# Gate-up weights of a mixture-of-experts kernel in blocks of 4 MB with runs of 32 KB per partition

## The chip, the cores and the metric

One core of a Trainium2 chip runs the whole program. The metric is the time of one execution on the device, in microseconds (us). "Before" and "after" are the kernel without and with the change.

## The reference, cut to what matters

One transformer layer on 256 tokens of 1024 features, all in float32. A token mixer (convolution branch, attention branch, gates, a merge) comes first; it ends in `x`. Then a mixture of experts reads the normalised `x`:

```python
logits = h @ w_router + b_router            # 32 experts
top_logits, top_idx = lax.top_k(logits, 4)  # 4 of them per token
gu = xb @ w_gate_up[e] + b_gate_up[e]       # (tokens, 1024) @ (1024, 2048)
glu = minimum(gu[:, ::2], 7); lin = clip(gu[:, 1::2], -7, 7)
act = glu * sigmoid(1.702 * glu) * (lin + 1)
y = act @ w_down[e] + b_down[e]             # (tokens, 1024) @ (1024, 1024)
```

The results are weighted, summed over a token's four experts, added to `x` and normalised. Every expert is worked on, so 8 MB of gate-up weights and 4 MB of down weights are read for each of the 32.

## The kernel before

**Stages.** Until about 290 us the mixer runs: TensorE multiplies weight chunks that SP streams through staging buffers. Then the experts follow one after the other, in pairs (`pair(m, last)`, L994, with `p` 0 and 1; expert number `i = 2m + p`). A program would add more rounds over the experts if one had over 64 tokens; register `final` (L536, L992) holds the last pair's number, 15 here.

**One expert on TensorE.** Gate-up (L999 to L1017) walks the 1024 features in eight steps `k` of 128. Two steps share one slot of 2 MB, so four slots j = 0 to 3 hold an expert's gate-up weights; after each slot the counter `up_used` goes up by one. Then come, for every second expert, the sum of two experts' rows into the output (`scatter`, L982), the gathering of the next expert's tokens (L955), its bias (L933), transposes of the activations (L1039) and of the gathered rows (`turn_gathered`, L963), and the product with the down weights (L1045 to L1055) from slots 4 and 5, with `down_used` counted. Which feature stands in which partition and step is the order of `PAIRS` (L66): the transposes L862, L967 and L694 read every second column, and `load_slot` (L432) gives partition p two neighbouring rows of the weights, a run of 16 KB.

**Slots.** There are ten slots of 128 partitions by 16 KB (L219): four for the gate-up weights of even experts, four for those of odd ones (`slot`, L372), two for down weights. They lie over buffers of the mixer, so the first loads wait until these are no longer needed (`EARLY`, L119, and L520 to L534). TensorE waits for a slot by its own semaphore (`wait_slot`, L376). ScalarE and VectorE work beside it (sigmoid L1250, clamps L1682 and L1684).

**The order of SP's queue.** SP issues every weight load and waits before each for the slot to be free. All transfers go through the one queue in the order of issue. `first_of_second(i)` (L547) issues the four gate-up loads of expert i + 2, each once expert i has used that slot; `rest_of_next(i)` (L538) issues the two down loads of expert i + 1, once expert i has used the down slots. For experts 0 to 16 the gate-up loads are issued first (L555 to L561), from 17 on the down loads (L562 to L569):

```python
first_of_second(2 * CATCH_UP, 0)      # CATCH_UP = 8
rest_of_next(2 * CATCH_UP, 0)
rest_of_next(2 * CATCH_UP + 1, 1)
first_of_second(2 * CATCH_UP + 1, 1)
```

**Other lines that the text speaks of.** ScalarE's queue loads the gate-up biases (L1205, four transfers, each 32 rows of 2 KB into 32 partitions) and the down biases (L1208, 32 rows of 4 KB into partitions 0 to 31). VectorE computes `final` in L1633 to L1639 and signals `routed`. Early in the program, VectorE computes the scalar `lam` in L1300 to L1303.

## Time and profile before

| | |
|---|---|
| median of three runs | 1215.8 us (1212.63 to 1217.0) |
| the profiled execution, its own time | 1212.78 us |
| its span in the profile | 1211.0 us |
| mean granted TensorE clock | 0.995 of full |

The page of the profile describes the one profiled execution, engine by engine, and the views behind it answer for a stretch, a line or an engine. In the stretches view each line is one stretch: its length, then busy us and number of instructions of TensorE's matmuls (PE), its weight loads (PEld), VectorE (DVE), ScalarE (ACT) and GpSimd (POOL), then the granted clock, the busy share of the 16 DMA engines (packets that lie across the ends of a stretch can lift it over 1), and GB/s. The span is 1.8 us shorter than that execution's time.

### The profile page before, as it was taken

What the parts mean: (1) busy time and instruction counts of PE and PEld (TensorE: products, weight loads), DVE (VectorE), ACT (ScalarE), POOL (GpSimd) and SP (SyncE); (2) the same over time, 40 slices, a digit from 0 to 9 for tenths busy, and PEclk for the clock granted to TensorE, in tenths of its full rate; (3) what the DMA queues carried; (4) which work ended last, traced back from release to release, by engine and by line L of the source; (5) the groups of instructions that cost most, each with busy time, mean ns of one, the idle gap of its engine ahead of it and who ended that gap; (6) DMA issues with size and microseconds to landing.
All of it is one profiled execution on the core that took longest, in us unless ns stands there. A gap on an engine that the chain in (4) does not pass through costs nothing.

```text
span 1211.0 us, 15215 instructions
## 1 busy us (share of the span) xinstructions
PE 1148.4 (95%) x6027; PEld 534.1 (44%) x6027; DVE 409.5 (34%) x795; ACT 208.7 (17%) x333; POOL 19.7 (2%) x40
## 2 busy tenths in 40 slices
PE   5999999999999999999999998989999999999997
PEld 4787899985333333333333332323333333333332
DVE  4447746663232222222222222222232222222222
ACT  4346543341011010101010101010110101010001
POOL 1000010000000000000000000000000000000000
PEclk9999999999999999999999999999999999999999
DMA  9997565798999999999999999999999999999994
GB/s 338 395 386 280 182 230 167 255 398 369 397 428 430 427 430 426 431 426 429 428 429 428 429 428 429 427 382 421 426 432 425 431 426 431 426 430 427 430 426 206
DMA packets 59394, 470.55 MB, mean 389 GB/s; under 512 B 5871, under 2 KB 11196, under 8 KB 32742
## 3 DMA queue, kind: packets, MB, share of 16 engines
q1 hardware_dynamic: 56644, 467.99, 93.5%
q10 hardware_dynamic: 2722, 2.16, 0.6%
q8 instruction: 20, 0.33, 0.1%
q14 instruction: 8, 0.07, 0.0%
HBM read 469.08 MB, written 1.06 MB: 388 GB/s over the span
## 4 chain that ended last, share of the span: by engine, by line
PE 65%; DMA 29%; DVE 2%; ACT 1%; SPq 1%; issue 1%; DVEq 0%; POOLq 0%; POOL 0%; ACTq 0%
PE ps L1014 19%; DMA expert<-in_w_down 16%; PE ps L783 15%; PE ps L1052 15%; DMA expert<-in_w_gate_up 12%; PE ps L988 4%; PE ps L959 2%; PE ps L727 1%; PE ps L658 1%; PE ps L940 1%; PE ps L1039 1%; ACT r_work L1254 1%; SPq L440 1%; DVE r_v L1691 1%; DMA ada_first<-in_w_ada 1%
## 5 line engine op out<-in xcount | busy, mean ns | idle before, releaser
L1014 PE MATMUL ps<-expert,r_work 128*64 128x512 f32 x2048 | 451.7, 594 | 12.3 <-DMA expert<-in_w_gate_up 11.3
L1014 PEld LDWEIGHTS ps<-expert,r_work 128*64 128x64 f32 x2048 | 146.5, 137 | 300.1 <-issue 280.1
L1052 PE MATMUL ps<-expert,r_work 128*64 128x512 f32 x1024 | 233.4, 606 | 24.1 <-DMA expert<-in_w_down 15.9
L1682 DVE TENSOR_SCALAR r_v<-ps 128x512 f32<-128x512 f32 x32 | 22.1, 692 | 371.3 <-PE ps L1014 371.3
L1052 PEld LDWEIGHTS ps<-expert,r_work 128*64 128x64 f32 x1024 | 72.8, 139 | 162.7 <-issue 136.9
L1250 ACT ACTIVATE r_v<-r_v 128x512 f32<-128x512 f32 x32 | 20.2, 630 | 713.8 <-DVE r_v L1682 713.8
L1702 DVE TENSOR_TENSOR r_work<-ps,r_gb 64x512 f32<-64x512 f32 x64 | 44.1, 689 | 169.5 <-PE ps L1052 169.0
L1364 DVE TENSOR_TENSOR w_lo<-stage,w_hi 128x2048 fp32r<-128x2048 f32 x36 | 82.2, 2289 | 55.9 <-ACT w_hi L1110 55.9
L783 PE MATMUL ps<-x_hi,w_hi 128*128 128x256 f32 x304 | 87.6, 288 | 0.0
L783 PE MATMUL ps<-x_lo,w_hi 128*128 128x256 f32 x304 | 86.0, 283 | 0.0
L783 PE MATMUL ps<-x_hi,w_lo 128*128 128x256 f32 x304 | 86.0, 283 | 0.0
L1110 ACT ACTIVATE w_hi<-stage 128x2048 fp32r<-128x2048 f32 x36 | 68.8, 1912 | 91.6 <-PE ps L783 68.9
L783 PEld LDWEIGHTS ps<-x_hi,w_hi 128*128 128x128 f32 x304 | 58.2, 191 | 11.6 <-issue 11.6
L959 PE MATMUL ps<-x_sb,r_work 128*64 128x512 f32 x256 | 61.2, 599 | 0.0
L988 PE MATMUL ps<-r_work 128*128 128x512 f32 x128 | 59.2, 605 | 0.0
L1623 DVE TENSOR_TENSOR r_work<-ps,small 128x256 f32<-128x256 f32 x64 | 26.9, 421 | 93.0 <-PE ps L967 93.0
L783 PEld LDWEIGHTS ps<-x_lo,w_hi 128*128 128x128 f32 x304 | 58.3, 192 | 0.0
L783 PEld LDWEIGHTS ps<-x_hi,w_lo 128*128 128x128 f32 x304 | 58.2, 192 | 0.0
L988 PEld LDWEIGHTS ps<-r_work 128*128 128x128 f32 x128 | 23.0, 189 | 35.9 <-issue 35.9
L940 PE MATMUL ps<-r_cu,r_work 32*64 32x512 f32 x256 | 34.8, 613 | 0.0
L959 PEld LDWEIGHTS ps<-x_sb,r_work 128*64 128x64 f32 x256 | 16.9, 136 | 39.7 <-issue 39.0
L1691 DVE TENSOR_TENSOR r_v<-r_v 128x512 f32<-128x512 f32 x32 | 33.6, 1049 | 1.1
(219 smaller groups left out, 862.3 us busy)
## 6 DMA issues: line engine op xcount, KB each, us to landing
expert<-in_w_gate_up SPq DMA_DIRECT2D x128, 2048.0 KB, 26.9
expert<-in_w_down SPq DMA_DIRECT2D x64, 2048.0 KB, 20.4
stage<-in_w_in SPq DMA_DIRECT2D x24, 1024.0 KB, 5.6
stage<-in_w_ada SPq DMA_DIRECT2D x16, 1024.0 KB, 7.7
ada_first<-in_w_ada SPq DMA_DIRECT2D x16, 256.0 KB, 6.4
ada_first<-in_w_ada SPq DMA_DIRECT2D x8, 512.0 KB, 12.2
stage<-in_w_o_attn SPq DMA_DIRECT2D x4, 1024.0 KB, 7.7
stage<-in_w_merge SPq DMA_DIRECT2D x4, 1024.0 KB, 5.8
```

Source lines behind the costliest of these rows:

```text
L783: m = pe.matmul(out_ap, lhs, rhs, start=first, stop=last, skip_group_check=True)
L940: pe.matmul(ps[CAP * g:CAP * g + CAP, j, :], sel[rows_of], bgu[rows_of, :], start=True, stop=False)
L959: mm = pe.matmul(ps[CAP * half:CAP * half + CAP, 2, :], g_hot[:, t, :], x_sb[:, t, 512 * half:512 * half + 512], start=(t == 0), stop=(t = ...
L988: pe.matmul(ps[:, 4 + 2 * t + half, :], st[:, t * P:t * P + P], y2[:, 512 * half:512 * half + 512], start=False, stop=False, skip_group_ch ...
L1014: mm = pe.matmul(ps[CAP * g:CAP * g + CAP, j, :], xg[:, 2 * (k % 4) + k // 4, :], buf[:, col:col + 512], start=False, stop=(k == KD - 1))
L1052: mm = pe.matmul(ps[CAP * half:CAP * half + CAP, 3, :], aT[:, ch, CAP * g:CAP * g + CAP], expert[n][:, col:col + 512], start=(q == 0), sto ...
L1110: act.activation(w_hi[n % 2], src, ACT.Copy).then_inc(hi_ready, 1)
L1364: v.tensor_tensor(w_lo[n % 2], src, w_hi[n % 2], ALU.subtract).then_inc(lo_ready, 1)
L1623: own.done(v.tensor_tensor(dst[:, qs], src[:, qs], per_chunk(a2, qs), ALU.mult))
L1682: v.tensor_scalar(glu.rearrange("p (b n) -> p b n", b=2), gu[:, :, :, 0], LIMIT, None, ALU.min).then_inc(glu_ready, 1)
L1691: v.tensor_tensor(act_sb.rearrange("p (c n) -> p n c", c=4), lin.rearrange("p (n c) -> p n c", c=4), sig.rearrange("p (n c) -> p n c", c=4 ...
L1702: ins = v.tensor_tensor(y2[CAP * p:CAP * p + CAP, 512 * half:512 * half + 512], ps[rows_in, 3, :], g2b[rows_in, 512 * half:512 * half + 51 ...
```

## The change

Slots that lie side by side in memory are joined to five blocks of 32 KB per partition. The features are dealt by fours: partition p of a block holds four neighbouring rows, 32 KB in one run. `load_block` loads a block with two transfers of 2 MB, one to partitions 0 to 63, one to partitions 64 to 127; each counts up the semaphore of one of the two slots. TensorE waits for both before the first step of a block, except in the last pair of experts. Loads by single slots remain for the gate-up weights of experts 0 to 3, 18 to 21, 30 and 31; all others (22 experts, 44 blocks) come by blocks. The order of gate-up and down loads changes over experts 17 to 19, one slot per expert. The first ten loads keep their waits, but which of them stands behind which wait is new. `lam` is computed later in VectorE's program. SP reads a second register value, which VectorE prepares before `routed`.

```diff
-PAIRS = [slice(2 * P * (k // 2) + k % 2, 2 * P * (k // 2) + 2 * P, 2) for k in range(4)]
+FOURS = [slice(k, 4 * P, 4) for k in range(4)]
...
-EARLY = {11: 0, 28: 1, 33: 2}
+EARLY = {11: 2, 28: 0, 33: 1}
+REST = [6, 3, 4, 5, 7, 8, 9]
...
-        order = [o_xn, o_bias, o_bp, o_oh, o_q, o_gate + 8192, in_order[1], o_w[0], o_w[2], o_hh]
-        expert = [at(f"expert{n}", o, 2 * SLOT) for n, o in enumerate(order)]
+        order = [o_bias, o_bp, o_xn, o_q, o_gate + 8192, in_order[1], o_oh, o_w[0], o_w[2], o_hh]
+        blocks = [at(f"expert{n}", order[2 * n], 4 * SLOT) for n in range(len(order) // 2)]
+        expert = [blocks[n // 2][:, 2 * SLOT * (n % 2):2 * SLOT * (n % 2) + 2 * SLOT] for n in range(len(order))]
+        assert all(order[n + 1] == order[n] + 8 * SLOT for n in range(0, len(order), 2))
...
                 if j < UP_SLOTS:
-                    src = w_gate_up[0, e, 2 * P * j:2 * P * j + 2 * P, :].rearrange("(p k) n -> p (k n)", k=2)
+                    d = 4 * P * (j // 2)
+                    src = w_gate_up[0, e, d:d + 4 * P, :].rearrange("(p h k) n -> p h (k n)", h=2, k=2)[:, j % 2, :]
...
+            def load_block(b, e, parity):
+
+                d = 4 * P * b
+                src = w_gate_up[0, e, d:d + 4 * P, :].rearrange("(p k) n -> p (k n)", k=4)
+                for part in range(2):
+                    n, rows_of = slot(2 * b + part, parity), slice(64 * part, 64 * part + 64)
+                    sp.dma_start(blocks[slot(2 * b, parity) // 2][rows_of, :], src[rows_of]).then_inc(slot_landed[n], 16)
...
-            for j in range(len(EARLY), NSLOT + TWICE):
-                if j == 3:
+            for n in REST:
+                if n == 6:
                     wait_product(sp, WO1, 1)
-                elif j == 4:
+                elif n == 3:
                     sp.wait_ge(m_lo, 4)
-                elif j == 5:
+                elif n == 4:
                     sp.wait_ge(m_ready, 4)
                     sp.wait_ge(lo_ready, STAGE_LAST[0] + 1)
-                elif j == 6:
+                elif n == 5:
                     sp.wait_ge(lo_ready, STAGE_LAST[2] + 1)
-                elif j == 7:
+                elif n == 7:
                     sp.wait_ge(half_done, 2 * (len(CHUNKS) - 1))
                 else:
                     wait_product(sp, MG1, 1)
-                load_slot(j % NSLOT, j // NSLOT, j // NSLOT)
+                load_slot(n % NSLOT, n // NSLOT, n // NSLOT)
             sp.wait_ge(routed, 1)
             final = sp.value_load(last_pair[0:1, 0:1], min_val=E // 2 - 1, max_val=ROUNDS * E // 2 - 1)
+            ahead_of_final = sp.value_load(last_pair[0:1, 1:2], min_val=E // 2 - 2, max_val=ROUNDS * E // 2 - 2)
...
             def first_of_second(i, parity):
 
-                for j in range(TWICE):
+                some_of_second(i, parity, 0, TWICE)
+
+            def blocks_of_second(i, parity):
+
+                for b in range(2):
+                    sp.wait_ge(up_used, UP_SLOTS * i + 2 * b + 2)
+                    load_block(b, (i + 2) % E, parity)
+
+            def some_of_second(i, parity, first, end):
+
+                for j in range(first, end):
                     sp.wait_ge(up_used, UP_SLOTS * i + (j + 1))
                     load_slot(j, (i + 2) % E, parity)
 
-            with sp.Fori(0, CATCH_UP) as m:
+            for p in range(2):
+                first_of_second(p, p)
+                rest_of_next(p, p)
+
+            with sp.Fori(1, CATCH_UP) as m:
                 for p in range(2):
-                    first_of_second(2 * m + p, p)
+                    blocks_of_second(2 * m + p, p)
                     rest_of_next(2 * m + p, p)
 
-            first_of_second(2 * CATCH_UP, 0)
-            rest_of_next(2 * CATCH_UP, 0)
-            rest_of_next(2 * CATCH_UP + 1, 1)
-            first_of_second(2 * CATCH_UP + 1, 1)
-
-            with sp.Fori(CATCH_UP + 1, final) as m:
+            for n in range(TWICE):
+                i, ahead = 2 * CATCH_UP + n, TWICE - n
+                some_of_second(i, n % 2, 0, ahead)
+                rest_of_next(i, n % 2)
+                some_of_second(i, n % 2, ahead, TWICE)
+
+            with sp.Fori(CATCH_UP + TWICE // 2, ahead_of_final) as m:
                 for p in range(2):
                     rest_of_next(2 * m + p, p)
-                    first_of_second(2 * m + p, p)
+                    blocks_of_second(2 * m + p, p)
+            for p in range(2):
+                rest_of_next(2 * ahead_of_final + p, p)
+                first_of_second(2 * ahead_of_final + p, p)
             rest_of_next(2 * final, 0)
...
-                    mm = pe.transpose(ps[:, 2, q * P:q * P + P], g_rows[:, PAIRS[q]], ident)
+                    mm = pe.transpose(ps[:, 2, q * P:q * P + P], g_rows[:, FOURS[q]], ident)
...
-                        if k % 2 == 0:
+                        if k % 4 == 0 or last and k % 2 == 0:
                             wait_slot(pe, k // 2, m, p)
+                        if k % 4 == 0 and not last:
+                            wait_slot(pe, k // 2 + 1, m, p)
...
-            v.wait_ge(lam_exp, 2)
-            own.done(v.tensor_tensor(lam_s[:, 4:5], lam_s[:, 3:4], lam_s[:, 2:3], ALU.subtract))
-            own.wait()
-            v.tensor_scalar(lam_s[:, 4:5], lam_s[:, 4:5], -LAM_INIT, None, ALU.add).then_inc(lam_out, 1)
-
             def bias_and_lam():
 
+                v.wait_ge(lam_exp, 2)
...
-            v.tensor_copy(last_pair[0:1, :], last_f[0:1, :]).then_inc(routed, 1)
+            own.done(v.tensor_scalar(over[:, 0:1], last_f, -1.0, None, ALU.add))
+            own.wait()
+            own.done(v.tensor_copy(last_pair[0:1, 0:1], last_f[0:1, :]))
+            own.done(v.tensor_copy(last_pair[0:1, 1:2], over[0:1, 0:1]))
+            own.wait()
+            v.tensor_copy(scrap[:, 2:3], ones[:, 0:1]).then_inc(routed, 1)
```

Not shown: the same exchange of `PAIRS` for `FOURS` in L688 and L863, the like dealing of the router's weights and of the second norm's gain (L1183 to L1186), the rest of the moved `lam` lines, `last_pair` with two columns instead of one, and the renamed cases of `early` (each buffer keeps the wait that it had).

## Rows read from the trace of the kernel before

**Rows 1.** The page: span, TensorE's busy time, GB/s by slice, SP's queue

```profile
span 1211.0 us, 15215 instructions
...
PE 1148.4 (95%) x6027; PEld 534.1 (44%) x6027; DVE 409.5 (34%) x795; ACT 208.7 (17%) x333; POOL 19.7 (2%) x40
...
GB/s 338 395 386 280 182 230 167 255 398 369 397 428 430 427 430 426 431 426 429 428 429 428 429 428 429 427 382 421 426 432 425 431 426 431 426 430 427 430 426 206
...
q1 hardware_dynamic: 56644, 467.99, 93.5%
```

**Rows 2.** The stretches view, two long stretches of the experts

```profile
330.00:780.00 450.00, 430.41 (x1980) 148.30 (x1978) 118.97 (x264) 39.45 (x56) 0.00 (x0) 0.99 1.01 429
985.00:1155.00 170.00, 157.38 (x730) 53.57 (x728) 42.42 (x96) 12.88 (x19) 0.00 (x0) 1.00 1.01 429
```

**Rows 3.** The page's instruction groups (busy us, mean ns) and transfer sizes

```profile
L1014 PE MATMUL ps<-expert,r_work 128*64 128x512 f32 x2048 | 451.7, 594 | 12.3 <-DMA expert<-in_w_gate_up 11.3
...
L1052 PE MATMUL ps<-expert,r_work 128*64 128x512 f32 x1024 | 233.4, 606 | 24.1 <-DMA expert<-in_w_down 15.9
...
expert<-in_w_gate_up SPq DMA_DIRECT2D x128, 2048.0 KB, 26.9
```

**Rows 4.** ScalarE's timeline: the sigmoid of four experts, start us first

```profile
443.22 0.63 ACT L1250 ACTIVATE r_v<-r_v 128x512 f32<-128x512 f32 x1 [22.24 <-DVE r_v L1682]
...
497.86 0.63 ACT L1250 ACTIVATE r_v<-r_v 128x512 f32<-128x512 f32 x1 [22.24 <-DVE r_v L1682]
...
1012.86 0.63 ACT L1250 ACTIVATE r_v<-r_v 128x512 f32<-128x512 f32 x1 [22.41 <-DVE r_v L1682]
...
1071.59 0.63 ACT L1250 ACTIVATE r_v<-r_v 128x512 f32<-128x512 f32 x1 [22.41 <-DVE r_v L1682]
```

**Rows 5.** TensorE's timeline in the last two experts

```profile
1150.39 3.65 PE L1014 MATMUL ps<-expert,r_work 128*64 128x512 f32 x16 [1.15 <-DMA expert<-in_w_gate_up]
1155.28 3.65 PE L1014 MATMUL ps<-expert,r_work 128*64 128x512 f32 x16 [1.24 <-DMA expert<-in_w_gate_up]
...
1193.46 7.09 PE L1052 MATMUL ps<-expert,r_work 128*64 128x512 f32 x32 [0.76 <-ACT r_work L1254]
```

**Rows 6.** SP's and TensorE's timelines where the load order changes

```profile
769.70 33.78 SPq L440 DMA_DIRECT2D expert<-in_w_down  x4
803.52 2.08 SPq L440 DMA_DIRECT2D expert<-in_w_gate_up  x4
...
794.60 3.65 PE L1052 MATMUL ps<-expert,r_work 128*64 128x512 f32 x16 [2.24 <-DMA expert<-in_w_down]
```

**Rows 7.** The stretches view, same columns, where the load order changes

```profile
795.00:811.00 16.00, 14.79 (x70) 4.79 (x68) 1.70 (x4) 0.00 (x0) 0.00 (x0) 1.00 0.87 341
820.00:835.00 15.00, 14.71 (x74) 5.11 (x72) 4.15 (x12) 1.19 (x2) 0.00 (x0) 1.00 0.99 409
```

**Rows 8.** The stretches view while 2 KB runs to 128 partitions are moved

```profile
187.00:189.00 2.00, 2.00 (x19) 2.00 (x18) 1.01 (x1) 0.96 (x1) 0.00 (x0) 1.00 1.05 409
```

**Rows 9.** The stretches view, the loads of L1205 and L1208 to 32 partitions each

```profile
189.20:189.60 0.40, 0.40 (x5) 0.40 (x5) 0.40 (x1) 0.26 (x1) 0.00 (x0) 1.00 0.99 226
189.60:190.00 0.40, 0.40 (x6) 0.40 (x5) 0.40 (x1) 0.34 (x1) 0.00 (x0) 1.00 0.91 287
```

**Rows 10.** Before the first expert: stretches view, VectorE's and SP's timelines

```profile
290.00:295.00 5.00, 5.00 (x24) 1.83 (x26) 2.20 (x9) 0.11 (x1) 0.00 (x0) 1.00 0.43 156
...
288.98 0.42 DVE L1623 TENSOR_TENSOR r_work<-ps,small 128x256 f32<-128x256 f32 x1 [3.07 <-PE ps L967]
...
268.23 36.23 SPq L440 DMA_DIRECT2D expert<-in_w_gate_up  x8
```

**Rows 11.** The DMA view, 330 to 370 us; last: us to landing

```profile
expert<-in_w_gate_up SPq DMA_DIRECT2D x6, 2048.0 KB, 16.3
```

**Rows 12.** Instructions by line and shape: weight loads of two transposes

```profile
L967 PEld LDWEIGHTS ps<-cst,r_cu 128*128 128x128 f32 x128 | 17.9, 206 | 0.5 <-ACT r_cu L1237 0.5
...
L636 PEld LDWEIGHTS ps<-cst,r_xn 128*128 128x128 f32 x16 | 3.0, 212 | 1.7 <-DVE r_xn L1273 1.7
```

More of the change, by code:

```diff
@@ L313, in block_kernel @@
         junk2 = r_cu[:, 0:512]
-        last_pair = at("last_pair", region(8), 1, I32)
+        last_pair = at("last_pair", region(8), 2, I32)
         ps = ctx.enter_context(nc.psum_tensor("ps", [P, 8, 512], F32))
@@ L506, in _ @@
                 early = EARLY.get(what[1]) if what[0] == "w" else None
-                if early == 0:
+                if early == 2:
                     sp.wait_ge(x_turned, 1)
@@ L510, in _ @@
                     sp.wait_ge(h_lo_ready, 3)
-                elif early == 1:
+                elif early == 0:
                     sp.wait_ge(scores_read, H)
                     sp.wait_ge(conv_lo, 1)
-                elif early == 2:
+                elif early == 1:
                     wait_product(sp, OC1, 1)
@@ L687, in mod_turn @@
                     row = mod[b][:, j * P:j * P + P]
-                    pick = mod[b][:, PAIRS[j]]
+                    pick = mod[b][:, FOURS[j]]
                     if b < 2:
@@ L862, in turn_x1 @@
                     mm = pe.transpose(ps[:, 2 + 2 * t + half, k * P:k * P + P],
-                                      x_sb[:, t, 512 * half:512 * half + 512][:, PAIRS[k]], ident)
+                                      x_sb[:, t, 512 * half:512 * half + 512][:, FOURS[k]], ident)
                 mm.then_inc(x1_turned, 1)
@@ L1182, in _ @@
                 if n == 5:
-                    act.dma_start(wr.rearrange("p (h s) n -> p h (s n)", s=2),
-                              w_router[0].rearrange("(h p s) n -> p h (s n)", p=P, s=2)).then_inc(wr_landed, 16)
-                    act.dma_start(g2n.rearrange("p (h s) -> p h s", s=2),
-                              dap(norm2_g, 0, [[2, P], [2 * P, KD // 2], [1, 2]])).then_inc(wr_landed, 16)
+                    act.dma_start(wr.rearrange("p (h s) n -> p h (s n)", s=4),
+                              w_router[0].rearrange("(h p s) n -> p h (s n)", p=P, s=4)).then_inc(wr_landed, 16)
+                    act.dma_start(g2n.rearrange("p (h s) -> p h s", s=4),
+                              dap(norm2_g, 0, [[4, P], [4 * P, KD // 4], [1, 4]])).then_inc(wr_landed, 16)
                     act.dma_start(brb, dap(b_router, 0, [[0, P], [1, E]])).then_inc(wr_landed, 16)
@@ L1298, in _ @@
                               ps[:, 2 + b, :].rearrange("p (k n) -> p k n", k=2)).then_inc(xT_dve, 1)
-            v.wait_ge(lam_exp, 2)
-            own.done(v.tensor_tensor(lam_s[:, 4:5], lam_s[:, 3:4], lam_s[:, 2:3], ALU.subtract))
-            own.wait()
-            v.tensor_scalar(lam_s[:, 4:5], lam_s[:, 4:5], -LAM_INIT, None, ALU.add).then_inc(lam_out, 1)
             def bias_and_lam():
+                v.wait_ge(lam_exp, 2)
+                own.done(v.tensor_tensor(lam_s[:, 4:5], lam_s[:, 3:4], lam_s[:, 2:3], ALU.subtract))
+                own.wait()
+                v.tensor_scalar(lam_s[:, 4:5], lam_s[:, 4:5], -LAM_INIT, None, ALU.add).then_inc(lam_out, 1)
                 v.wait_ge(g_made, 1)
@@ L1638, in _ @@
             own.wait()
-            v.tensor_copy(last_pair[0:1, :], last_f[0:1, :]).then_inc(routed, 1)
+            own.done(v.tensor_scalar(over[:, 0:1], last_f, -1.0, None, ALU.add))
+            own.wait()
+            own.done(v.tensor_copy(last_pair[0:1, 0:1], last_f[0:1, :]))
+            own.done(v.tensor_copy(last_pair[0:1, 1:2], over[0:1, 0:1]))
+            own.wait()
+            v.tensor_copy(scrap[:, 2:3], ones[:, 0:1]).then_inc(routed, 1)
             v.wait_ge(gather_done, 1)
```

## The prediction, made before the changed kernel was run

> **What bounds the kernel.** I read the page first. TensorE is busy 95% of the span, which looks like the bound, but the GB/s line stands at 425 to 432 in nearly every slice from the twelfth to the last but one, and SP's queue moves 468 MB in 93.5% of the span [rows 1]. Two resources are nearly full, so the stretches view has to say which one waits. In both long stretches of the experts the 16 DMA engines are busy at 1.01 and move 429 GB/s [rows 2]: they never pause. The cadence of experts shows TensorE's side. Two experts take 497.86 - 443.22 = 54.6 us while TensorE draws on ten filled slots, and 1071.59 - 1012.86 = 58.7 us later [rows 4]. Two experts need 12 transfers of 2.097 MB; at 429 GB/s that is 12 x 4.89 = 58.7 us. So the later cadence is the DMA's, and TensorE alone could do 54.6. TensorE's timeline agrees: in expert 30 it waits 1.15 and 1.24 us before single slots of gate-up weights, while the down product of expert 31 starts on an activation, not on a transfer [rows 5]. The end of the kernel therefore hangs on the time at which the loads for expert 30 land, plus TensorE's work behind it. A microsecond won or lost on the queue before that point counts in full; a microsecond of TensorE's does not, as long as the 4.1 us per pair between the cadences are there.
>
> **Part 1, the turn of the load order.** SP's timeline has one group of four down loads that lasts 33.78 us, from 769.70 [rows 6]: the two down loads of expert 17 are followed by those of expert 18, which must wait for a whole expert, and all gate-up loads stand behind them. The queue runs empty. From 795 to 811 us the rate is 341 GB/s instead of 429: 16 x (429 - 341) / 429 = 3.3 us lost. From 820 to 835 it is 409: another 0.7 us [rows 7]. TensorE waits 2.24 us for a down load there [rows 6]. The change moves only one gate-up load per expert behind the down loads. Then between two down loads of consecutive experts at least one 4.89 us transfer is issued each time and no gap of an expert's length is left with only two loads in it. I take back all 4.0 us; the ends are 0 (the idle moves elsewhere) and 4.0.
>
> **Part 2, runs of 32 KB.** What does a run cost beside its bytes? With 2 KB runs to all 128 partitions the engines move 409 GB/s at a share of 1.05, so 389 at full share [rows 8]; that is 16 x 2048 / 389 = 84 ns per run and engine. With 16 KB runs it is 429 GB/s [rows 2], or 16 x 16384 / 429 = 611 ns. A line through both has 36.8 ns per 1000 bytes (527 ns for 14336 bytes) and leaves 84 - 75 = 9 ns per run. A block of 4 MB is 16 runs per engine now and 8 after the change: 8 x 9 = 72 ns saved of 9.8 us. There are 22 experts with two blocks each: 44 x 0.072 = 3.2 us. The number of transfers stays the same (two per block), so nothing else is saved. Bounds: nothing, if a 32 KB run is carried as two; 6.3 us, if it cost nothing beside its bytes. I take 3.2, the line's own value.
>
> **Part 3, coarser waits.** SP now waits until two slots are used before it issues either, which delays the first of them by one slot's product: 16 matmuls in 3.65 us [rows 5]. This costs nothing while the queue holds more than that: a 2 MB transfer takes 4.89 us but lands a median 16.3 us after issue between 330 and 370 us, where the first blocks are issued [rows 11], and 26.9 over the kernel [rows 3]. The cover is thinnest at the start, and there experts 0 and 1 keep single slots. If the cover were gone, each block would cost up to 3.65 us. On TensorE the two waits per block replace four single ones; it starts up to 4.89 us later and then runs two slots through, so it ends a gate-up product at most 3.65 us later. In the DMA-bound stretch this delays only the release of slots, again under the queue's cover. Behind TensorE's wait stand ScalarE and VectorE, which have nothing else to do. In experts 30 and 31, where the end is set, waits are single as before. So 0.
>
> **Part 4, start of the experts.** The ten first loads keep the moments of issue: each position of SP's list has the same wait as before, only slot 3 stands where slot 4 stood, and slot 5 where slot 6 stood. The last of them are issued from 268.23 on [rows 10], expert 0 needs slot 3 after some ten us of product and slot 5 only for its down product, so no wait appears. What matters here is when expert 0 starts, because the queue stands still for lack of free slots just then: 156 GB/s between 290 and 295 us [rows 10]. VectorE's way to `routed` gets four more small operations and two waits, but behind it VectorE sits idle for 3.07 us until 288.98, when the gathered rows have been turned [rows 10]; and SP's second register read falls in the same gap, ahead of its first free slot; 0. The transposes read every fourth column instead of every second. Weight loads with every second column take 206 ns, contiguous ones 212 [rows 12], so a stride has cost nothing so far; I take 0. Were a stride of four to double them, the 12 transposes ahead of expert 0 would add up to 2.5 us, and in the later experts it would be TensorE's slack. The moved `lam` lines let VectorE skip two one-element operations at the start; I count nothing for them.
>
> **Sum.** -4.0 - 3.2 = -7.2 us against the profiled execution's own 1212.8 us: 1205.6. The median of the runs is 3.0 us above that execution, so in its terms 1215.8 - 7.2 = 1208.6 us. No change can be told here from one below about 0.5%, or 6.1 us; the forecast lies just past it.
>
> **Rival 1, the queue at half rate.** The change replaces transfers over all partitions by transfers over 64. The only rows with less than 128 are the loads of L1205 and L1208: while the engines are busy at 0.99 with 32-partition transfers, they move 226 GB/s [rows 9], against 389 to 409 just before [rows 8]. So busy engines can be slow, and the cause could be how few partitions they write into at once. If every half block ran at 226 GB/s, it would take 9.28 us instead of 4.89: 88 x 4.39 = 386 us, less the 4.0 of part 1, or 1598 us. It decides from the first blocks, near 350 us, and the queue, already the bound, hides none of it. Against it speaks the next stretch: where the two loads overlap, one to the upper and one to the lowest partitions, the rate is 287 at a share of 0.91, or 315 [rows 9]. Two halves stand directly behind each other in the queue and there is no wait between them. An engine that is ahead works on the less crowded half and should run faster there, which takes it further ahead, until both halves are in use at the same time and the rate is whole again. That is my reason to make this a rival and not the forecast; it is an inference from two short stretches. The Trainium skill speaks for the rival: "SBUF — State Buffer", section on the DMA port swizzle, says that partitions 0 to 63 reach only 8 of 16 ports, and that two transfers to the two halves serialize. By its 8 x 27.2 = 218 GB/s a half block would take 9.6 us, and my estimate by this page is 1630 us. Rows 9 agree with it for 32 partitions; no row shows 64. Chance 0.19.
>
> **Rival 2, slow until the engines have spread.** The same mechanism, but the spreading takes time, or is partial. Each expert loaded at half rate costs 4 x 4.39 = 17.6 us. Three such experts: 53 - 7.2 = +46, about 1262 us. This is the case that ends slower without a collapse: from 1222 (a single expert's worth or less) to 1300 (five). For it: the engines finish each transfer at nearly the same time now, as the even rate of rows 2 suggests. Chance 0.19.
>
> **Rival 3, the change does less than it says.** A 32 KB run is carried as two of 16 KB, or the idle of the turn reappears at another expert. With one of the two gone the time is 1211.8 or 1212.6; with a slower start by the bound of part 4 beside it 1213 to 1217. All this lies within 0.5%. For it: both savings are small sums of small prices, 9 ns per run above all. Against it: the empty queue in rows 7 is plain. Chance 0.22.
>
> **How the numbers follow.** Forecast 0.40, rival 3 0.22, rival 2 0.19, rival 1 0.19. The first is the chance of faster by over 0.5%, the second that of within 0.5%, the last two together, 0.38, are slower. The forecast's own range is 1203 (both savings at their upper bounds, 1215.8 - 10.3 = 1205.5, less 2.5 for the spread of the runs) to 1212. To leave out no more than 2 in 10 I reach over rivals 3 and 2 to 1300 and leave out the full half rate.
>
> **What would show it.** Right: the rate between 350 and 1150 us is about 431 GB/s, no slice near 800 is below 420, SP's timeline has no group of four down loads, the late cadence of a pair is about 58.4 us (58.7 less four blocks' 0.29), TensorE's waits for gate-up weights come twice an expert and last up to 3 us. Rival 1: the share of busy engines stays at 1.0 and the rate of experts 4 to 29 falls to about 268 GB/s (12.58 MB in 37.1 + 9.8 us), with a landing time above 40 us. Rival 2: low rates near 350 us that recover. Rival 3: rate unchanged at 429, or a new dip. The forecast is wrong if the rate falls while the engines are busy.

## The result, and the profile after the change

The changed kernel takes 1836.15 us (median of 4 runs, 1821.68 to 1864.39) against 1216.3 us before (4 runs, 1212.63 to 1217.0). The ratio is 1.506, with an interval of 1.500 to 1.512, taken without the slow run of 1864.39 us. The forecast was 1208.6 us with a range of 1203 to 1300. The profiled execution took 1828.34 us.

The page of the changed kernel, with the lines that answer to [rows 1] and [rows 3]:

```profile
span 1826.5 us, 15129 instructions
...
PE 1245.2 (68%) x6027; PEld 557.1 (30%) x6027; DVE 411.0 (22%) x798; ACT 208.4 (11%) x333; POOL 19.7 (1%) x40
...
GB/s 360 383 259 202 207 338 373 395 250 225 227 244 235 236 237 235 212 235 240 231 234 220 205 213 283 349 380 355 254 234 220 242 228 230 211 201 213 299 221 195
...
q1 hardware_dynamic: 51012, 467.99, 92.4%
...
L1047 PE MATMUL ps<-expert,r_work 128*64 128x512 f32 x2048 | 483.7, 629 | 181.8 <-DMA expert<-in_w_gate_up 180.9
...
L1085 PE MATMUL ps<-expert,r_work 128*64 128x512 f32 x1024 | 295.5, 735 | 373.7 <-DMA expert<-in_w_down 368.4
...
expert<-in_w_gate_up SPq DMA_DIRECT2D x128, 2048.0 KB, 59.5
```

SP's queue moves the same 468 MB and is still busy 92% of the span, which has grown by half. The 16 DMA engines are not idle, they are slow. TensorE's waits for weights are 181 + 368 = 549 us, where they were 11 and 16. A transfer takes 59.5 us from issue to landing instead of 26.9.

The stretches view of the changed kernel, columns as in [rows 2]; the last two are the busy share of the 16 DMA engines and GB/s:

```profile
340.00:360.00 20.00, 20.00 (x94) 6.89 (x91) 3.20 (x10) 0.00 (x0) 0.00 (x0) 1.00 1.08 410
360.00:400.00 40.00, 32.22 (x154) 11.43 (x152) 12.97 (x31) 4.93 (x7) 0.00 (x0) 0.95 0.97 206
400.00:450.00 50.00, 31.82 (x128) 10.55 (x128) 7.18 (x16) 1.82 (x3) 0.00 (x0) 0.81 1.00 244
800.00:1000.00 200.00, 108.69 (x448) 35.31 (x445) 25.56 (x55) 8.67 (x12) 0.00 (x0) 0.76 1.00 229
1000.00:1100.00 100.00, 42.40 (x167) 13.58 (x165) 11.85 (x29) 4.30 (x6) 0.00 (x0) 0.70 1.00 208
1100.00:1200.00 100.00, 82.84 (x356) 27.42 (x357) 19.30 (x39) 6.16 (x9) 0.00 (x0) 0.90 0.92 337
1200.00:1300.00 100.00, 89.55 (x420) 31.63 (x421) 26.72 (x62) 8.64 (x12) 0.00 (x0) 0.97 0.94 327
1300.00:1400.00 100.00, 60.47 (x246) 20.23 (x242) 14.88 (x33) 4.93 (x7) 0.00 (x0) 0.83 1.00 245
1600.00:1700.00 100.00, 60.64 (x234) 20.33 (x234) 13.48 (x31) 4.93 (x7) 0.00 (x0) 0.81 0.92 204
```

The rate is still 410 GB/s while the last single slots are loaded and breaks down to 206 within 20 us, with SP's first block (issued at 352.76). It recovers to 337 and 327 only between 1100 and 1300 us, where the gate-up weights of experts 18 to 21 come by single slots, and falls again with the next blocks. Two things are to be seen. Busy engines at half the rate are rival 1 of the prediction. And within each group of experts the rate sinks further, 244 to 208 and 245 to 204, which no case of the prediction had.

ScalarE's timeline (start us first), the sigmoids of experts 3, 4, 16, 17, 21, 22 and 29:

```profile
389.41 0.63 ACT L1283 ACTIVATE r_v<-r_v 128x512 f32<-128x512 f32 x1 [22.24 <-DVE r_v L1719]
434.88 0.63 ACT L1283 ACTIVATE r_v<-r_v 128x512 f32<-128x512 f32 x1 [40.47 <-DVE r_v L1719]
...
1121.19 0.63 ACT L1283 ACTIVATE r_v<-r_v 128x512 f32<-128x512 f32 x1 [55.35 <-DVE r_v L1719]
1166.28 0.63 ACT L1283 ACTIVATE r_v<-r_v 128x512 f32<-128x512 f32 x1 [38.13 <-DVE r_v L1719]
...
1278.00 0.63 ACT L1283 ACTIVATE r_v<-r_v 128x512 f32<-128x512 f32 x1 [22.24 <-DVE r_v L1719]
1326.79 0.63 ACT L1283 ACTIVATE r_v<-r_v 128x512 f32<-128x512 f32 x1 [43.78 <-DVE r_v L1719]
...
1750.06 0.63 ACT L1283 ACTIVATE r_v<-r_v 128x512 f32<-128x512 f32 x1 [55.38 <-DVE r_v L1719]
```

The same timeline of the kernel before, the sigmoids of experts 3, 17, 21 and 29:

```profile
388.57 0.63 ACT L1250 ACTIVATE r_v<-r_v 128x512 f32<-128x512 f32 x1 [22.24 <-DVE r_v L1682]
...
788.80 0.63 ACT L1250 ACTIVATE r_v<-r_v 128x512 f32<-128x512 f32 x1 [22.92 <-DVE r_v L1682]
...
901.47 0.63 ACT L1250 ACTIVATE r_v<-r_v 128x512 f32<-128x512 f32 x1 [22.24 <-DVE r_v L1682]
...
1130.33 0.63 ACT L1250 ACTIVATE r_v<-r_v 128x512 f32<-128x512 f32 x1 [22.41 <-DVE r_v L1682]
```

The 14 experts 4 to 17, loaded by blocks, take 1166.28 - 389.41 = 776.9 us, the 8 experts 22 to 29 take 1750.06 - 1278.00 = 472.1. That is 1249 us for 22 experts, 56.8 each. Before, the same experts took 400.2 + 228.9 = 629.1 us, 28.6 each. So they take 620 us more, and the span has grown by 615.5. Experts 18 to 21 take 25 to 29 us as before. The whole loss lies in the experts that are loaded by blocks.

### The profile page after: what moved, and what is told of

It is laid out like the page before. It is cut to its first block, busy times and chain, and to the rows that moved or that the text cites. A ratio compares the mean times of both kernels' runs of the same rounds, so it can differ in the third digit from the quotient of the medians.

```text
span 1826.5 us, 15129 instructions
## 1 busy us (share of the span) xinstructions
PE 1245.2 (68%) x6027; PEld 557.1 (30%) x6027; DVE 411.0 (22%) x798; ACT 208.4 (11%) x333; POOL 19.7 (1%) x40
## 4 chain that ended last, share of the span: by engine, by line
PE 51%; DMA 26%; another core or an unknown queue 19%; DVE 2%; ACT 1%; issue 1%; SPq 0%; DVEq 0%; POOLq 0%; POOL 0%; ACTq 0%
DMA expert<-in_w_down 24%; PE ps L1047 18%; PE ps L1085 13%; PE ps L814 10%; PE ps L1019 2%; DMA expert<-in_w_gate_up 2%; PE ps L990 1%; PE ps L758 1%; PE ps L689 1%; PE ps L1072 1%; PE ps L971 1%; ACT r_work L1287 1%; DVE r_v L1728 1%; DVE r_v L1725 0%
## 5 line engine op out<-in xcount | busy, mean ns | idle before, releaser
L1047 PE MATMUL ps<-expert,r_work 128*64 128x512 f32 x2048 | 483.7, 629 | 181.8 <-DMA expert<-in_w_gate_up 180.9
L1085 PE MATMUL ps<-expert,r_work 128*64 128x512 f32 x1024 | 295.5, 735 | 373.7 <-DMA expert<-in_w_down 368.4
L1047 PEld LDWEIGHTS ps<-expert,r_work 128*64 128x64 f32 x2048 | 156.9, 145 | 493.5 <-issue 493.5
L1085 PEld LDWEIGHTS ps<-expert,r_work 128*64 128x64 f32 x1024 | 85.0, 168 | 561.3 <-DMA expert<-in_w_down 389.7
L1655 DVE TENSOR_TENSOR r_work<-ps,small 128x256 f32<-128x256 f32 x64 | 26.9, 421 | 92.6 <-PE ps L998 92.6
L1715 DVE COPY r_work<-ps 128x256 f32<-128x256 f32 x16 | 6.8, 425 | 100.8 <-PE ps L1037 100.8
## 6 DMA issues: line engine op xcount, KB each, us to landing
expert<-in_w_gate_up SPq DMA_DIRECT2D x128, 2048.0 KB, 59.5
```

Of the source, the lines that this page charges most:

```text
L1047: mm = pe.matmul(ps[CAP * g:CAP * g + CAP, j, :], xg[:, 2 * (k % 4) + k // 4, :], buf[:, col:col + 512], start=False, stop=(k == KD - 1))
L1085: mm = pe.matmul(ps[CAP * half:CAP * half + CAP, 3, :], aT[:, ch, CAP * g:CAP * g + CAP], expert[n][:, col:col + 512], start=(q == 0), sto ...
L1655: own.done(v.tensor_tensor(dst[:, qs], src[:, qs], per_chunk(a2, qs), ALU.mult))
```

## The experiments

The theory after the result: a transfer that writes only into the lower or the upper 64 partitions runs at half rate, whatever its neighbours in the queue. It leaves open whether the number of partitions, their place, the 32 KB run or the order does it, whether the two parts of the change gave what was forecast, and why the rate sinks further within a group of experts.

### Nine ways to load a block, with nothing computed

Five buffers of 32 KB per partition are filled in turn from the gate-up weights, 15 blocks of 4 MB (14 in the seventh way) for each way of loading; nothing is computed. Four of the ways, cut from the program; each pair in brackets is one transfer, its partitions and its columns. `A` is all 128 partitions, `LO` and `HI` are the lower and the upper 64, `C0` and `C1` the first and the second 16 KB of a partition, `ALL` both:

```python
                take(sp, n, [(A, C0), (A, C1)], slots)
...
                take(sp, n, [(A, ALL)], whole)
...
                take(sp, n, [(LO, ALL), (HI, ALL)], halves)
...
                take(sp, n, [(slice(0, 127, 2), ALL), (slice(1, 128, 2), ALL)], steps)
```

> The whole layer is left out: nothing is computed, the output is zeros, and only weights are loaded, in nine streams of 15 blocks of 4 MB each (the seventh 14), each stream kept five blocks deep with no compute engine beside it. The streams are, in order: two slots over all partitions (16 KB runs); one transfer over all partitions (32 KB runs); halves of partitions with 32 KB runs (low, high); halves with 16 KB runs; every second partition, 32 KB runs; two blocks in halves then one over all partitions, as in the changed kernel; halves grouped low, low, high, high; quarters of 32 partitions (first, third, second, fourth); halves again, low half from SP's queue and high half from ScalarE's. Theory P (a transfer over half the partitions gets half the rate): 429, 431, 218 to 230, 218 to 230, then with every second partition between 218 and 429, the mix about 260, grouped 218 to 230, quarters 218 to 230, and with two queues well above 230 because both halves are written at once. Theory R (32 KB runs are slow whatever the partitions): second, third, fifth to ninth stream all near 230, the fourth stream 429. Theory O (transfers are fine, the changed kernel's order and waits starve them): all streams 425 to 432. My failed step, that engines spread over the halves by themselves, would show as a rate in stream three that starts low and climbs.

The stretches view of this run (columns: GpSimd's busy time, granted clock, share, GB/s), in this order: slots, whole blocks, halves (early part, later part), halves with 16 KB runs, every second partition, the mix of the changed kernel, halves in the order lower, lower, upper, upper, quarters of 32 partitions (first, third, second, fourth), and halves from the queues of SP and ScalarE at once:

```profile
5.00:145.00 140.00, 0.00 (x0) 1.00 1.01 429
155.00:290.00 135.00, 0.00 (x0) 1.00 1.00 432
320.00:420.00 100.00, 0.00 (x0) 1.00 1.00 209
460.00:560.00 100.00, 0.00 (x0) 1.00 1.00 210
605.00:890.00 285.00, 0.00 (x0) 1.00 1.01 215
900.00:1040.00 140.00, 0.00 (x0) 1.00 1.00 431
1050.00:1290.00 240.00, 0.00 (x0) 1.00 1.00 243
1305.00:1575.00 270.00, 0.00 (x0) 1.00 1.00 208
1590.00:1870.00 280.00, 0.00 (x0) 1.00 1.01 213
1890.00:2160.00 270.00, 0.00 (x0) 1.00 1.00 219
```

Halves move 209 GB/s and stay there over 15 blocks: nothing spreads. The run length is not the cause (215 with 16 KB), nor is the order (208 and 213), nor is one queue (219 with two). Sixty-four partitions are not the cause either: every second partition gives 431. It is the place. Theory P of the expectation, which went by the number of partitions, missed on two of the ways: it had two queues well above 230 and every second partition below 429.

The Trainium skill, "SBUF — State Buffer", section on the DMA port swizzle, says that partitions 0 to 63 reach 8 of 16 ports, 218 GB/s; this run agrees with 209 to 219. By the map of ports in that section of the Trainium skill the even partitions reach all 16 ports, and so do the odd ones; 431 agrees with that.

A mix with two blocks in three by halves would move 3 / (2/209 + 1/429) = 252 GB/s if each kept its own rate. The line above has 243, but its stretch begins and ends inside halves; from 1100 to 1200 us, two whole rounds of the mix, the same view gives 251. The low stretches of the changed kernel, 204 to 229, lie clearly below the sum.

### One part of the change at a time

Three kernels: the changed one with whole blocks in one transfer (SP counts the second slot's semaphore itself), the changed one with blocks loaded slot by slot, and the kernel before with nothing but the new load order.

```diff
-                for part in range(2):
-                    n, rows_of = slot(2 * b + part, parity), slice(64 * part, 64 * part + 64)
-                    sp.dma_start(blocks[slot(2 * b, parity) // 2][rows_of, :], src[rows_of]).then_inc(slot_landed[n], 16)
+                first, second = slot(2 * b, parity), slot(2 * b + 1, parity)
+                sp.dma_start(blocks[first // 2][:, :], src).then_inc(slot_landed[first], 16)
+                sp.sem_inc(slot_landed[second], 16)
```

> The changed kernel with each block of 4 MB loaded by one transfer over all 128 partitions (32 KB runs kept); SP counts up the second slot's semaphore itself. Theory P: the loss goes away and what is left is the forecast's sum, 1216.3 - 7.2 = 1209 us (1205 to 1213), rate in the block stretches 431 GB/s, clock 0.99. Theory R: stays near 1836 us with about 230 GB/s. Theory O: stays above 1400 us with idle DMA engines.

```diff
-                    n, rows_of = slot(2 * b + part, parity), slice(64 * part, 64 * part + 64)
-                    sp.dma_start(blocks[slot(2 * b, parity) // 2][rows_of, :], src[rows_of]).then_inc(slot_landed[n], 16)
+                    load_slot(2 * b + part, e, parity)
```

> The changed kernel with each block loaded as two slots over all partitions, 16 KB runs; the pairwise waits, the turn over three experts, the dealing by fours and the moved lines stay. All theories but O: 1216.3 - 4.0 = 1212.3 us (1210 to 1216), the difference to the whole blocks is the price of the runs, 3.2 us. Theory O: far above 1216.

```diff
-            first_of_second(2 * CATCH_UP, 0)
-            rest_of_next(2 * CATCH_UP, 0)
-            rest_of_next(2 * CATCH_UP + 1, 1)
-            first_of_second(2 * CATCH_UP + 1, 1)
+            for n in range(TWICE):
+                i, ahead = 2 * CATCH_UP + n, TWICE - n
+                some_of_second(i, n % 2, 0, ahead)
+                rest_of_next(i, n % 2)
+                some_of_second(i, n % 2, ahead, TWICE)
```

> The kernel before with only the load order turned over three experts instead of one. From rows: 4.0 us of idle queue near 800 us go, 1216.3 - 4.0 = 1212.3 us. If the idle only moves: 1216. Neither P, R nor O speaks to it; it prices part 1 of the sum alone.

| kernel | median us | ratio to before, interval |
|---|---|---|
| before, same chip | 1215.26 (15 runs) | |
| new load order alone | 1210.99 (8 runs) | 0.9959, 0.9944 to 0.9973 |
| changed, loads slot by slot | 1211.10 (8 runs) | 0.9966, 0.9954 to 0.9978 |
| changed, whole blocks in one transfer | 1208.18 (6 runs) | 0.9941, 0.9927 to 0.9956 |

The stretches view of the kernel with the new load order alone, where the order turns [rows 7]:

```profile
795.00:811.00 16.00, 14.06 (x60) 4.57 (x62) 3.99 (x12) 1.17 (x1) 0.00 (x0) 0.89 1.01 429
```

The stretches view of the kernel with whole blocks:

```profile
340.00:780.00 440.00, 424.70 (x1942) 146.05 (x1940) 113.50 (x253) 36.35 (x52) 0.00 (x0) 0.98 1.00 431
```

The hole of 341 GB/s is gone, and the new order alone gives 1210.99 - 1215.26 = -4.3 us. Slots to whole blocks is 1208.18 - 1211.10 = -2.9 us, with the rate up from 429 to 431. Between the new order alone and the changed kernel loaded slot by slot stand the dealing by fours, the waits for pairs of slots, the other slots and SP's second register: +0.1 us for all. The intervals of the three ratios leave out 1, but they are 3 us wide, so each single term is known to about 2 us only.

### The same two transfers, by even and odd partitions

The sharpest test of the place: the changed kernel with the same number of transfers, bytes, runs, semaphores and order, and only the partitions of each half dealt otherwise.

```diff
-                    n, rows_of = slot(2 * b + part, parity), slice(64 * part, 64 * part + 64)
+                    n, rows_of = slot(2 * b + part, parity), slice(part, 127 + part, 2)
```

> The changed kernel with one thing exchanged: the two transfers of a block go to the even and to the odd partitions instead of the lower and the upper 64. Runs, bytes, number of transfers, semaphores and waits stay. Theory P as I first put it (few partitions are slow) says about 1600 to 1836 us. Theory P' (the slow thing is that all engines write into the same half of the partitions; the stream with every second partition ran at 431 GB/s) says 1216.3 - 7.2 = 1209 us, like the whole blocks.

The stretches view of this kernel:

```profile
340.00:780.00 440.00, 425.04 (x1940) 146.60 (x1938) 114.29 (x257) 36.34 (x52) 0.00 (x0) 0.98 1.00 431
```

1207.80 us (5 runs, 1206.25 to 1210.23), a ratio of 0.9935 (0.9922 to 0.9949) to the 1215.91 of before on that chip. One slice expression takes away more than 620 us and leaves a kernel that beats both. It can't be told apart from the one with whole blocks; either is the version to keep. So the place of the partitions is the cause of the whole loss: nothing else differs between this kernel and the changed one.

### Why the rate sinks: is it TensorE?

While the changed kernel loads blocks, TensorE's granted clock is 0.70 to 0.83 in the stretches above from 400 us on, a mix of its levels of 2.4 and 1.2 GHz. After a wait of 22.82 us a group of 16 matmuls of the down product takes 6.28 us, where it took 3.65 [rows 6]. TensorE's timeline, changed kernel:

```profile
1028.68 6.28 PE L1085 MATMUL ps<-expert,r_work 128*64 128x512 f32 x16 [22.82 <-DMA expert<-in_w_down]
```

To see whether this slower TensorE holds the slots, 7 of the 16 groups of gate-up matmuls of each expert are left out; every transfer stays.

```diff
-                        for j in range(2):
+                        for j in range(2 if k == KD - 1 else 1):
```

> The changed kernel with 7 of 16 gate-up matmul groups left out (the second 512 columns of all but the last step), transfers unchanged. Theory T: TensorE's work bounds part of the time, since it ran at half clock for long stretches; leaving out about 6 us of full-clock work per expert (12 at half clock) would take 100 to 250 us off the 1836. Theory D: the queue alone sets the time, the result stays within 40 us of 1836, the late stretch included.

The stretches view of this kernel:

```profile
400.00:500.00 100.00, 49.73 (x194) 16.11 (x194) 14.86 (x33) 4.93 (x7) 0.00 (x0) 0.74 1.01 241
1000.00:1100.00 100.00, 32.29 (x134) 10.77 (x130) 13.48 (x31) 4.93 (x7) 0.00 (x0) 0.66 0.94 211
```

1846.31 us (4 runs; three within 1844.29 to 1849.6, one at 1759.07). With almost half of the gate-up product gone, three runs, the profiled one among them, still have the time of the changed kernel, and the rates are its own too: 241 and 211 GB/s where it had 244 and 208. So TensorE's work and its late release of slots are not what makes the rate sink. The fourth run is 77 us below the changed kernel's median, more than the 40 of theory D and less than the 100 of theory T; it has no profile, and why it was faster stays open. It also shows that the total of a single run says little here.

### Why the rate sinks: engines out of step

The next theory (D in the expectations): the 16 DMA engines get out of step with each other, and the mix of halves and full transfers is then slower still. In its first form the engines drift apart by themselves. To test that, the mix runs alone and for long: 66 blocks, nothing computed.

> The whole layer is left out, the output is zeros: one stream of 66 blocks in the pattern two blocks in lower and upper halves, one block as two slots over all partitions, with no compute engine at work. It asks why the changed kernel's blocks ran at 208 to 244 GB/s overall, below the 252 that 209 for halves and 429 for the rest would give. Theory D (the 16 engines drift apart over many transfers and the loads over all partitions then collide with late halves): the rate starts near 243 and falls towards 210 to 230 within a millisecond, though no TensorE is there. Theory T (TensorE at half clock holds slots too long): it stays at 243 to 252.

```profile
50.00:400.00 350.00, 0.00 (x0) 1.00 1.00 251
750.00:1090.00 340.00, 0.00 (x0) 1.00 1.01 248
```

These two lines of its stretches view show no fall to speak of, where theory D had 210 to 230 within a millisecond. Its first form is refuted: alone, the mix keeps the 252 of the sum above, and the fall needs something that the kernel adds. In a second run of this kind, of 60 blocks, unevenness is added: ahead of blocks 12, 24, 36 and 48 a small transfer of 4 partitions. The trace has four packets of 32 KB for each of them, so at most four of the 16 engines carry one.

```diff
+            def push(n):
+                sp.wait_ge(pushed, 16 * push_count[0])
+                push_count[0] += 1
+                sp.dma_start(aside[0:4, :], src_of(n)[0:4, :]).then_inc(pushed, 16)
...
+                if n and n % 12 == 0:
+                    push(n)
```

> Nothing is computed. 60 blocks of 4 MB are loaded in the mix of the changed kernel (two blocks by halves of the partitions, then one as two transfers over all partitions). Ahead of blocks 12, 24, 36 and 48 one more small transfer is issued, 4 partitions of 32 KB, which gives a few of the 16 engines extra work and so puts the engines out of step with each other. Theory D (in the kernel the other, uneven transfers put the engines out of step, and engines that are out of step share the halves worse in this mix): the rate falls from phase to phase, from 250 GB/s in the first 12 blocks to 210 to 235 GB/s in the last 12, and the whole takes over 1060 us. Rival N (being out of step costs nothing, or is healed by the next full transfer): 247 to 251 GB/s in every phase, a dip of a few us at each small transfer at most, and 1010 to 1025 us for the whole. Rival S (out of step is the way to the spread that the prediction spoke of): the rate rises with each phase, to over 270 GB/s.

The stretches view of this run, between the issue of one small transfer and the next. A small transfer moves only when the queue has come to it, some 80 us after its issue, so a stretch still begins at the rate of the one before:

```profile
50.00:100.00 50.00, 0.00 (x0) 1.00 1.01 251
150.00:330.00 180.00, 0.00 (x0) 1.00 1.01 239
380.00:560.00 180.00, 0.00 (x0) 1.00 1.01 221
600.00:820.00 220.00, 0.00 (x0) 1.00 1.00 200
870.00:1200.00 330.00, 0.00 (x0) 1.00 0.96 178
```

Four transfers of 128 KB, each 0.3 us at 429 GB/s, cost some 200 us: 1215.82 us in all, against the 1019.35 of the control below. From line to line the rate falls by another 12 to 22 GB/s, at full busy share until the last stage, and it does not come back within this run. The expectation had the direction, but not the size: 210 to 235 at the end, where 178 was measured. As a control the same bytes over all 128 partitions, 1 KB each, so that every engine has the same extra work:

```diff
-        aside = nc.alloc_sbuf_tensor("aside", [4, 8192], F32)
-                    sp.dma_start(aside[0:4, :], src_of(n)[0:4, :]).then_inc(pushed, 16)
+        aside = nc.alloc_sbuf_tensor("aside", [P, 256], F32)
+                    sp.dma_start(aside[:, :], src_of(n)[:, 0:256]).then_inc(pushed, 16)
```

> The run of the pushed loads once more, but each of the four small transfers has the same 128 KB as 128 partitions of 1 KB, so that all 16 engines get the same work. Theory D (what harms is that the engines are out of step): 247 to 251 GB/s throughout, as without the small transfers, and about 1015 us in all. Rival I (any transfer in between harms): the rate falls as with the uneven ones, to under 200 GB/s in the last fifth, and about 1216 us in all.

```profile
400.00:600.00 200.00, 0.00 (x0) 1.00 1.00 251
600.00:800.00 200.00, 0.00 (x0) 1.00 1.00 245
800.00:1000.00 200.00, 0.00 (x0) 1.00 1.01 247
```

1019.35 us, and 245 to 251 GB/s in its stretches. So it is the unevenness, not the extra transfer. Last, the test in the kernel: one wait between experts 11 and 12 lets the queue run dry, so that all engines start again together.

```diff
-            with sp.Fori(1, CATCH_UP) as m:
+            some_experts(1, 6)
+            for n in range(NSLOT + TWICE):
+                sp.wait_ge(slot_landed[n], 16 * (13 if TWICE <= n < NSLOT else 7))
+            some_experts(6, CATCH_UP)
```

> The changed kernel, with one wait more: between experts 11 and 12 SP waits until all issued loads of weights have landed before it issues the next, so the 16 engines start again together. Undisturbed, the changed kernel moves 229 GB/s from 800 to 1000 us and 208 from 1000 to 1100, and its sigmoids of experts 13 to 16 stand 60.4 to 61.8 us apart. Theory D (the engines get out of step with each other, and the queue is slower for it): after the wait the rate is back at 240 to 250 GB/s for 100 us or more, the experts behind it take 50 to 56 us, and in spite of the 10 to 30 us that the empty queue costs the kernel is not slower, or some us faster than 1836. Rival W (the low rate comes from something else that grows with the experts, as TensorE's halved clock or other transfers): rates of 208 to 229 GB/s and 60 to 62 us per expert as before, and 10 to 30 us more in all.

The stretches view of this kernel; SP issues again at 970.13 us:

```profile
400.00:450.00 50.00, 32.23 (x128) 10.55 (x128) 6.61 (x14) 1.82 (x3) 0.00 (x0) 0.83 1.01 243
700.00:800.00 100.00, 43.03 (x164) 13.46 (x166) 9.05 (x19) 3.11 (x4) 0.00 (x0) 0.69 1.01 205
950.00:1000.00 50.00, 29.43 (x134) 10.22 (x130) 10.45 (x27) 3.71 (x5) 0.00 (x0) 0.81 0.66 146
1010.00:1100.00 90.00, 57.92 (x250) 19.37 (x250) 14.86 (x33) 4.93 (x7) 0.00 (x0) 0.82 1.01 255
1200.00:1300.00 100.00, 98.68 (x452) 34.31 (x450) 23.85 (x52) 6.75 (x10) 0.00 (x0) 0.99 1.01 430
1600.00:1700.00 100.00, 61.83 (x247) 20.92 (x245) 14.87 (x33) 4.93 (x7) 0.00 (x0) 0.81 1.01 251
```

Ahead of the wait the rate sinks as in the changed kernel, in this run earlier. From the new start to the end it is 249 to 255 with blocks and 430 with single slots, where the changed kernel had 204 to 245 and 327. ScalarE's timeline has the last eight experts with blocks 49.7 us apart in the mean, as 12.58 MB at 252 GB/s would have it. TensorE's clock is 0.69 to 0.83 ahead of the wait and 0.79 to 0.83 with blocks behind it, so the clock doesn't make the difference. The kernel takes 1780.81 us in its one run, 41 us below the fastest of the changed kernel's four (1821.68), although it has a wait more and empties the queue once.

The step itself can be read from the traces. For each weight transfer they have 16 moments at which the slot's semaphore is counted up by one; no view prints them, but they lie in the packed trace. There are as many as DMA engines (the small transfers of four packets have 5 each), so I read them as one engine's share landed at each. The time from the first to the last is then the gap between the engines. Medians over the transfers that end in a stretch, beside the rate there:

| kernel | stretch, us | gap, us | GB/s |
|---|---|---|---|
| before | 340 to 360 | 2.1 | |
| before | 1000 to 1100 | 1.5 | 429 |
| even and odd partitions | 985 to 1155 | 1.5 | 430 |
| changed | 340 to 360, ahead of the first block | 1.8 | 410 |
| changed | 400 to 450 | 5.6 | 244 |
| changed | 800 to 1000 | 20.9 | 229 |
| changed | 1000 to 1100 | 39.2 | 208 |
| changed | 1250 to 1300, at the end of the single slots | 5.6 | |
| changed | 1600 to 1700 | 43.2 | 204 |
| drained | 700 to 800 | 31.0 | 205 |
| drained | 1010 to 1100, behind the wait | 0.9 | 255 |
| drained | 1600 to 1700 | 0.8 | 251 |

The gap grows while the rate sinks, shrinks while single slots are loaded, and is gone behind the wait. At its widest it is one engine above all: of a transfer of the changed kernel that lands from 1606 us on, 15 engines are done within 8.7 us and the last one after 44.4. TensorE and SP wait for the full count of 16, so each slot waits for the last engine.

The traces also narrow down what starts it. A gap of about 2 us is there ahead of the first block, in the kernel before as well, so it does not come from the blocks but from something ahead of them. With transfers over all partitions it stays at 2 us; with halves it grows; and from the 0.9 us behind the wait it did not grow in the 800 us that followed, most of them with halves. Two things stay open: which transfer makes the first gap (none was taken away), and by what mechanism halves widen it and pull the rate even below that of halves alone, 178 against 209 GB/s.

## Why the prediction was wrong, point by point

**What bounds the kernel** was right, and it is why the loss came through in full: the queue was at 1.01 with 4 us of slack per pair behind it, and hid nothing.

**Part 1** was right: -4.0 forecast, -4.3 measured (known to about 2 us), and the dip of [rows 7] is gone: 429 GB/s where it was 341. **Part 2** had the right price for the run: -3.2 forecast, -2.9 from slots to whole blocks, which also have one transfer less per block; the two transfers by even and odd partitions end within 0.4 us of the whole blocks, on another chip. A 32 KB run is not carried as two: the trace of the changed kernel has packets of 32768 bytes. But the change as written doesn't get this saving, because its runs come in halves of the partitions. **Parts 3 and 4** were right at 0: +0.1 us together. (Part 4 says that only two slots are loaded later than before. Slots 0, 1 and 4 also move back by one place; it made no wait that shows: expert 0's sigmoid starts at 305.55 us, 0.8 later than before.) Weight loads with a stride of four take 207 ns, those with a stride of two took 206 [rows 12]. The forecast of 1208.6 is the time of the change without its halves: 1208.2 and 1207.8 us were measured.

**The step that failed** stands in rival 1: "An engine that is ahead works on the less crowded half and should run faster there, which takes it further ahead, until both halves are in use at the same time and the rate is whole again." No row showed that an engine gets ahead, nor that it would then be faster. The halves alone stay at 209 GB/s from the first block to the last. Where engines do get apart the rate falls: from 251 to 178 when they are pushed apart, and from 244 to 208 in the changed kernel, while the gap grows from 5.6 to 39 us. The sign of the argument was wrong. It came from two stretches of 0.4 us [rows 9], the first of which, 226 GB/s at 0.99, had been the nearest measurement of the new operation. Half rate, the price of that nearest row, should have stood as the main case, and the argument from the second stretch, where a share of 0.91 could mean many things, as the doubt about it. **Rival 2** rested on the same spreading and falls with it: the low rates near 350 us came, and they did not recover but sank.

**Rival 1** had the effect, half rate at a full busy share, and was given 0.19. As its cause it named how few partitions are written at once; the runs show that the place counts and not the number, and of the prediction only the sentence on the Trainium skill had that. Its time, 1598 us, is 238 too low, for three reasons. The rate of halves is 209, not 226: 2.097 MB take 10.03 us, and 88 x (10.03 - 4.89) = 452 instead of 386, or 66 us. Engines out of step: 22 experts take 1249 us instead of 22 x 49.9 = 1098, with 12.58 MB at 252 GB/s in 49.9 us; that is 151. And the sum adds the dearer transfers to experts of 29.35 us, the queue's own time, while these 22 took 28.6 on slots filled ahead; that is another 17. The last 4 us are within the spread of the runs. Of the signs that it named, the share near 1.0 (0.92 to 1.01) and the landing time above 40 us (59.5) are there; the 268 GB/s came out as 204 to 245.

**Rival 3** did not come true for either saving: without the halves both are there, -4.3 and -2.9 us.

## What to carry to other kernels

When a transfer is split in two, split it so that each part still touches the whole range of partitions (even and odd, or columns), or don't split it. The lower or the upper 64 partitions alone had half the rate in each order and queue that was tried. When a change replaces the one operation that the bound resource does all day, load a few blocks in the new way with nothing else around, before reasoning about how it might balance itself. And where busy DMA engines lose rate from stage to stage, look how far apart the 16 counts of one transfer's semaphore land, and let the queue run dry once to see whether the rate comes back.

## What the hardware showed that was not expected

- The lower and the upper half of the partitions take 208 to 219 GB/s from busy DMA engines, even when both halves are in flight from two queues; 64 alternating partitions take 431.
- In a mix of halves and full transfers, four uneven transfers of 128 KB took the rate from 251 to 178 GB/s; the same bytes spread evenly left it at 245 to 251. In the kernel the engines came up to 40 us and more apart, and one drain of the queue brought the gap to 0.9 us and the rate from 205 back to 255.
- A gap of 2 us between the engines stayed at 2 us for 800 us of transfers over all partitions, and grew to 39 us in 700 us with halves among them.
- An estimate: a run costs about 9 ns beside its bytes. 429 GB/s with 16 KB and 432 with 32 KB runs give it, and so did the line through 2 KB and 16 KB.
- TensorE's clock fell to a mean of 0.7 among waits of 20 us and more, and a group of 16 matmuls went from 3.65 to 6.28 us. It cost nothing that shows: with 7 of 16 gate-up groups left out, three runs of four took as long.
